# A two-layer block kernel on one core: gate tiles dealt 3, 2, 2, 1 between attention scores, and a first expert step whose rows TensorE picks

## The reference, cut to what matters

```python
def second_block(x, mem, ...):
    h = rmsnorm_2(x, norm_mix_g[l])
    u_glu, q, k, v, f_logit, gate_c, gate_a = jnp.split(h @ w_in[l], cuts, axis=-1)
    conv_out = conformer_conv(u_glu, ...)            # ends in silu(layernorm(u)) @ pw_w
    logf = jax.nn.log_sigmoid(f_logit + fox_bf[l])
    attn = fox_attention(q, k, v, logf)              # 8 heads of 64, causal, with a decay
    merged = sigmoid(gate_c) * conv_out + sigmoid(gate_a) * (attn @ attn_branch_w[l])
    x = x + merged @ w_out[l]
    x = x + cross_attention(...)
    x = x + hierarchical_moe(rmsnorm_2(x, norm_moe_g[l]), ...)

def fox_attention(...):
    s = q_i @ kh.T * scale + c_i[:, None] - c[None, :]     # c: running sum of logf
    p = softmax(where(kpos <= qpos, s, -inf))
    o = p @ vh

def hierarchical_moe(h, ...):      # 16 experts in 4 groups, two experts for each token
    combine = one_hot(expert_idx) * weights
    u = silu(h @ w_gate[e]) * (h @ w_up[e]) * combine      # w_gate, w_up: 1024 x 256
    y = sum over e of u @ w_down[e]                        # w_down: 256 x 1024
```

## Time and profile before

| | us |
|---|---|
| median of 3 runs | 1931.56 (1930.52 to 1934.93) |
| the profiled execution | 1928.75 |
| its span (first to last instruction) | 1927.0 |

### The profile page before, as it was taken

One profiled execution on the slowest core, in us unless ns is written; L12 is line 12 of the kernel. 1 busy time (PEld: TensorE's weight loads), 2 busy tenths in 40 slices (PEclk: granted clock), 3 DMA queues, 4 the chain that ended last, 5 costly groups with the idle time before them and its releaser, 6 DMA issues. The chain is left out here.

```text
span 1927.0 us, 18124 instructions
## 1 busy us (share of the span) xinstructions
PE 1730.1 (90%) x6987; PEld 788.3 (41%) x6987; DVE 554.9 (29%) x1088; ACT 385.4 (20%) x700; POOL 24.0 (1%) x34
## 2 busy tenths in 40 slices
PE   6998999999989999999999899978999999457882
PEld 4544545554436443444443334423444334212220
DVE  4605403551124011101111159553110113410113
ACT  5102113431022110010100310166300112300112
POOL 0100000000000000000000000000000000100001
PEclk9998999999999999999999999989999999778996
DMA  9611364111323999999999803111112131489965
GB/s 368 240 44 44 110 218 174 45 66 46 129 87 133 409 419 423 425 421 420 421 422 425 308 2 129 44 44 44 44 44 87 54 120 66 162 253 361 306 212 182
DMA packets 97193, 383.05 MB, mean 199 GB/s; under 512 B 11284, under 2 KB 11620, under 8 KB 86628
## 3 DMA queue, kind: packets, MB, share of 16 engines
q1 hardware_dynamic: 87268, 350.14, 47.3%
q10 hardware_dynamic: 5824, 17.30, 2.9%
q0 software_dynamic: 4032, 14.68, 2.0%
HBM read 467.03 MB, written 18.87 MB: 252 GB/s over the span
## 5 line engine op out<-in xcount | busy, mean ns | idle before, releaser
L1738 PE MATMUL bank<-H,weight_slots 128*128 128x512 f32 (+1 forms) x1024 | 424.4, 575 | 4.1 <-ACT H L677 2.9
L1738 PEld LDWEIGHTS bank<-H,weight_slots 128*128 128x128 f32 x1024 | 197.4, 194 | 226.0 <-issue 220.3
L1738 PE MATMUL bank<-R,weight_slots 128*128 128x512 f32 x576 | 250.9, 594 | 4.4 <-DVE R L1285 2.1
L1738 PEld LDWEIGHTS bank<-R,weight_slots 128*128 128x128 f32 x576 | 108.4, 190 | 143.2 <-issue 133.8
L2064 PE MATMUL bank<-weight_slots,SM 128*64 128x512 f32 x640 | 143.9, 595 | 9.4 <-DMA weight_slots<-in_w_up_e 9.4
L2390 PE MATMUL bank<-weight_slots,SM 128*32 128x512 f32 x768 | 98.3, 659 | 34.2 <-DMA weight_slots<-in_expert_w_up 33.4
L2092 PE MATMUL bank<-weight_slots,SM 128*64 128x512 f32 x384 | 113.7, 604 | 3.4 <-DMA weight_slots<-in_w_down_e 3.4
L1738 PE MATMUL bank<-R 128*128 128x128 f32 (+2 forms) x720 | 95.8, 286 | 3.5 <-ACT R L964 2.0
L1738 PEld LDWEIGHTS bank<-R 128*128 128x128 f32 x720 | 87.0, 195 | 6.9 <-issue 4.4
L2064 PEld LDWEIGHTS bank<-weight_slots,SM 128*64 128x64 f32 x640 | 45.4, 137 | 104.3 <-issue 84.2
L1738 PE MATMUL bank<-weight_slots,H 128*128 128x512 f32 x192 | 82.9, 592 | 0.0
(11 more groups left out here) (419 smaller groups left out, 1525.1 us busy)
## 6 DMA issues: line engine op xcount, KB each, us to landing
weight_slots<-in_expert_w_gate SPq DMA_DIRECT2D x102, 512.0 KB
weight_slots<-in_expert_w_up SPq DMA_DIRECT2D x102, 512.0 KB
R<-in_expert_w_down SPq DMA_DIRECT2D x51, 1024.0 KB
weight_slots<-in_w_up_e SPq DMA_DIRECT2D x24, 2048.0 KB, 17.3
weight_slots<-in_w_down_e SPq DMA_DIRECT2D x24, 2048.0 KB, 23.7
weight_slots<-in_w_in SPq DMA_DIRECT2D x18, 2048.0 KB, 10.2
weight_slots<-in_w_gate_e SPq DMA_DIRECT2D x16, 2048.0 KB, 17.0
weight_slots<-in_w_ada SPq DMA_DIRECT2D x12, 2048.0 KB, 10.6
```

The source lines that it names most:

```text
L1738: ins = nc.tensor.matmul(dst, lhsT, rhs, start=(i == 0), stop=(i == len(pairs) - 1))
```

## The change

Attention: the gate tiles are dealt otherwise among the pairs, on PE and on ACT alike, and both ends of the convolution move one pair later. Experts: the rows of step 0 are no longer read back from `x_rows`; PE picks and transposes them in one, as products of `h2_stage` with a table of zeros and ones that DVE makes from the slots (`pick_rows`). `load_rows(0)` goes. The list `rows_in` is rearranged so that nothing lands in `h2_stage`'s memory early.

```diff
@@ ScalarE
                 if hp + 1 < FOX_H // 2:
                     cb_copy(hp + 1)
+                    if hp == 0:
+                        gate_c(0)
                     probs(hp + 1)
+                    gate_c(2 * hp + 1)
+                    gate_c(2 * hp + 2)
                 else:
                     scale_probs(FOX_H * TT - 1)
-                gate_c(2 * hp)
-                gate_c(2 * hp + 1)
+                    gate_c(2 * hp + 1)
...
-                if hp == 1:
+                if hp == 2:
                     conv_silu()
...
-            for q in range(4):
+            for q in range(1, 4):
                 load_rows(q)
@@ VectorE
-                if hp == 1:
+                if hp == 2:
                     norm_conv()
...
+            step(nc.vector.tensor_tensor(pos_in, pos2.unsqueeze(3).broadcast_to([P, 2, TT, NSLOT]),
+                                         column_row.unsqueeze(1).unsqueeze(1).broadcast_to([P, 2, TT, NSLOT]), ALU.subtract))
+            in_block = iota[:, 0:BLK].unsqueeze(1).unsqueeze(1).broadcast_to([P, TT, NSLOT, BLK])
+            for a, rows in enumerate((first_rows, second_rows)):
+                nc.vector.tensor_tensor(rows.rearrange("p t (c r) -> p t c r", c=NSLOT), in_block, pos_in[:, a, :, :].unsqueeze(3).broadcast_to([P, TT, NSLOT, BLK]),
+                                        ALU.is_equal).then_inc(sem("first_hits"), 1)
+            dve.wait_ge(sem("first_hits"), 2)
+            nc.vector.tensor_tensor(first_rows, first_rows, second_rows, ALU.add).then_inc(sem("first_hits"), 1)
@@ TensorE
                     decays(hp + 1)
                     logits(hp + 1, (0, 1))
-                    if hp == 0:
-                        gate_c(1)
+                    gate_c(2 * hp + 1)
                     logits(hp + 1, (2, 3))
-                if hp:
-                    gate_c(2 * hp)
+                    gate_c(2 * hp + 2)
+                else:
                     gate_c(2 * hp + 1)
                 pe.wait_ge(sem("P_ready"), 8 * (hp + 1))
...
+            def pick_rows():
+                pe.wait_ge(*reached("h_rows", TT))
+                pe.wait_ge(sem("first_hits"), 3)
+                for i in range(2):
+                    for k in range(4):
+                        c = 128 * (4 * i + k)
+                        ins = product(PS[i][:, 128 * k:128 * (k + 1)], [(h2_stage[:, t, c:c + 128], first_rows[:, t, :]) for t in range(TT)])
+                    ins.then_inc(sem("q_turn_x"), 1)
...
-            turn_rows(0)
+            pick_rows()
@@ tables
-        rows_in = [a[:, D * i:D * (i + 1)] for a, n in ((R5, 2), (R6, 4), (h_flat[:, 4096:6144], 2), (x_flat, 4)) for i in range(n)]
+        rows_in = [a[:, D * i:D * (i + 1)] for a, n in ((R5, 2), (h_flat[:, 4096:6144], 2), (x_flat, 4), (R6, 4)) for i in range(n)]
```

More of the change, by code:

```diff
@@ L104 @@
 SHARED = {"product_done": bases(PRODUCT_STAGES), "copy_done": bases(COPY_STAGES), "vector_done": bases(VECTOR_STAGES)}
-CONST = {"ident": 0, "ones": 128, "s_le_j": 256, "s_ge_j": 384, "future": 512, "dft": 640, "iota": 896, "pick": 960, "fold": 962, "desc": 982, "column": 986, "first": 990, "thresh": 994, "both_norms": 1010, "final_norm": 1011, "eps2": 1012}
-NCONST = 1013
+CONST = {"ident": 0, "ones": 128, "s_le_j": 256, "s_ge_j": 384, "future": 512, "dft": 640, "iota": 896, "pick": 960, "fold": 962, "desc": 982, "column": 986, "first": 990, "thresh": 994, "both_norms": 1010, "final_norm": 1011, "eps2": 1012, "column_row": 1013}
+NCONST = 1017
 def constant_tables():
@@ L135, in constant_tables @@
     table[:, 1012] = EPS * EPS
+    table[:, 1013:1017] = BLK * NQUAD * other
     n, m = np.arange(T // 2)[:, None], np.arange(T)[None, :]
@@ L372, in build @@
         column, first, thresh = (const[:, CONST[n]:CONST[n] + k] for n, k in (("column", NG), ("first", NSLOT), ("thresh", T // BLK)))
+        column_row = const[:, CONST["column_row"]:CONST["column_row"] + NSLOT]
+        pos_in = R7[:, 2256:2256 + 2 * TT * NSLOT].rearrange("p (a t c) -> p a t c", a=2, c=NSLOT)
+        first_rows = R7[:, 3072:3072 + T].rearrange("p (t s) -> p t s", t=TT)
+        second_rows = R7[:, 3584:3584 + T].rearrange("p (t s) -> p t s", t=TT)
         desc = const[:, CONST["desc"]:CONST["desc"] + 4].unsqueeze(1).broadcast_to([P, TT, 4])
@@ L2365, in _ @@
             ins.then_inc(sem("rank_mm"), 1)
+            def pick_rows():
[6 more added lines that the diff above has]
+                    ins.then_inc(sem("q_turn_x"), 1)
             def turn_rows(q):
-                pe.wait_ge(sem(f"rows_in{q % 4}"), 16 * NSLOT * (q // 4 + 1))
+                pe.wait_ge(sem(f"rows_in{q % 4}"), 16 * NSLOT * (q // 4 + (1 if q % 4 else 0)))
                 for i in range(2):
```

## The result

| | us |
|---|---|
| before, median of 4 runs | 1933.24 (1930.52 to 1936.82) |
| after, median of 4 runs | 1909.18 (1905.75 to 1914.79) |
| ratio | 0.9877, 95% interval 0.9847 to 0.9907 |
| profiled executions, before and after | 1928.75 and 1908.44 (spans 1927.0 and 1906.7) |

The change takes 24 us off the median (18 to 30), where 26.6 had been forecast. Between the two profiled executions it is 20.3 us. In a later job, beside the experiments, the same kernel had 1912.96 (4 runs) against 1933.55 (9 runs): 0.9902, 0.9873 to 0.9932.

The account below looks back on a forecast made before the run. TensorE's waits in the attention and the step-to-step chain at the experts' start were taken as the bound; 19.2 us plus 7.4 make 26.6, from median 1931.56 to 1904.9 us, own range 1901 to 1910, wider range 1898 to 1915.

Parts of the forecast that it names:

- clock rival: Attention: the granted clock falls in the new stalls, two to four costing 2.2 to 3.8 us each; 1909 to 1920, chance 0.14.
- Pair 0: Attention, first pair: value part starts 1.6 us earlier behind gate tile 2, and runs warm, 2.2 us shorter.
- Pairs 1 and 2, up to the value part: Attention: 20.5 us from one value part to the next, gaining 1.6 and 7.5 us, with a 1.9 us stall.
- Pairs 1 and 2, the value part: Attention: the value part was taken at 8.53 us, with no loss of clock in the sum.
- Pair 3: Attention, last pair: one gate tile instead of two, 8.4 us against 14.7, gaining 6.3; sigmoid covered by 1.2 us.
- The prediction's last sentence: Signs of being wrong: clock falling at stalls, gate tile 7 waiting for ACT, or step 1's weights not equally earlier.
- Table switches: ScalarE in the attention: each table load costs 1.28 us, the next activation 0.01 us behind, without further drain.
- the rival that rested on it: ScalarE in the attention: each exposed table switch drains 1.38 us more, 8.5 us in all; 1913, chance 0.05.
- Experts, the start: Second experts: pick of 7 to 14 us, tables 2.4 us later, first gate_up 7.4 us earlier, 20.7 behind the slots.
- Experts, the end: Second experts: the start's whole 7.4 us reaches the end, bounds 1.9 and 8.8.
- From then on all is a chain: Experts after the first gate_up: gate_up, load, gate_up move along together, keeping the 7.4 us.
- the rival of the late weights: Experts: step 0's weights come with the last of the backlog, gaining 1.9 us instead of 7.4; 1910.4, chance 0.10.

Follow-up runs that it names:

- attn_only: The kernel before with only the attention part of the change; 1916.13 us against 1935.62, ratio 0.9898.
- conv_moved: The kernel before with only the convolution's two ends (norm on VectorE, silu on ScalarE) one pair later, gate tiles unchanged; 1930.07 us against 1935.62, ratio 0.9967.
- experts_only: The kernel before with only the experts part of the change; 1923.68 us, ratio 0.9937.

## Why the prediction was right

The forecast of 26.6 us stands against 24 (18 to 30) and, in the later job, 19 (13 to 25). The direction held, and the stalls and the early start came at the places that were named; the sum was too high in both halves. The trace gives the attention 15.3 us where 19.2 had been forecast (13.5 in attn_only), and the experts 6.2 us in the profiled pair, 2.4 in the mean of all traces, where 7.4 had been. Between the profiled executions that is 20.3 us, so that the median came as near as 24 is in part luck. The measured 1909.18 also lies in both the forecast's own range (1901 to 1910) and that of the clock rival (1909 to 1920), and the first of the prediction's signs of being wrong, a fall of the granted clock at the stalls, did come.

*Pair 0.* 1.6 and 2.2 us forecast. From gate tile 1 to the value part it is 18.92 us instead of 20.36, 1.4; the value part took 8.54 instead of 10.69, 2.15. Both held.

*Pairs 1 and 2, up to the value part.* 1.6 and 7.5 us forecast; from the end of one value part to the start of the next it is 20.58 us both times, against 22.07 and 28.05: 1.5 and 7.5. The stall was 1.92 as written. The split that the prediction gives for its 7.5 doesn't hold: both orders have two gate tiles there, none fewer. By the rows it is 3.5 us of stalls (4.13, 0.58 and 0.73 less 1.92) and 3.9 us that scores and gate tiles no longer lose at the low clock (16.10 us for two tiles before, 14.2 after). Up to 3.0 of it comes from conv_silu alone, as conv_moved showed.

*Pairs 1 and 2, the value part.* Here a term was missing from the sum. I took 8.53 us, and it is 10.23 and 10.26, since the clock fell: 1.7 us each. It was a rival (two to four stalls that cost 2.2 to 3.8 us each, chance 0.14) and came true at two of the stalls, at the smaller price of 1.7. The argument against it, that pair 0 had had a much longer stall, was no argument, because pair 0 had lost 2.2 us to it.

*Pair 3.* 6.3 us forecast, 14.73 to 8.56 measured: 6.2. Gate tile 7 waited for the copy of bank 5 (0.69), and the cover of ScalarE's sigmoid was 1.44 us where I had 1.2. The prediction's last sentence names this wait as a sign of being wrong, while its own working has it; it cost nothing beyond the sum.

*Table switches.* The rows after show the load of 1.28 us and the activation 0.02 us behind it (1291.61, 1292.91), as those before. The Trainium skill, "ScalarE: Activation LUTs", section "What ACT_TABLE_LOAD costs", adds 1.38 us of drain to each. At these switches the trace doesn't show it; the rival that rested on it (1913 us) is refuted here by the pairs' times, which fit without it, and ScalarE isn't idle ahead of the load either: its last scaling ends where the load starts.

*Experts, the start.* The first gate_up 20.7 us behind the slots was forecast, 20.8 came, and 20.7 to 21.9 in six more traces. The pick took 10.20 us between the bounds of 7 and 14. The tables came 2.15 us later behind the slots, SyncE's first load 2.3, against 2.4.

*Experts, the end.* "From then on all is a chain" is the step that was too strong. In the profiled pair 4.8 us of the lead arrived at the last gate_up (the 6.2 at the end hold 1.4 us that lie behind it), over all traces 2.4. The bounds (1.9 to 8.8) hold this, and the rival of the late weights (1.9 us, chance 0.10) came half true: not the first half of step 0's weights but the second was caught in the backlog. I had read one window of DMA share 0.18 and taken the engines to be idle from there on; their share was 0.88 again 10 us later and 0.93 to 1.03 after that. That the profiled pair came so near to the 7.4 was luck: the trace of after has one of the earliest ends of the seven, and that of before the latest of the three.

What stays open: why the medians of the parts add to more than the whole, and how much of the experts' gain is the earlier start. Executions of one kernel differ by 4 to 12 us, so four runs may be all there is to the first; it wasn't tested. This spread goes with TensorE's clock: of 29 executions of the kernel before in the three jobs of the experiments, the four under 1928 us had a mean granted clock of 0.957 to 0.960, the others (from 1930.44) 0.951 to 0.956.

## What to carry to other kernels

Idle time ahead of a stretch is not worth its length alone: count the clock with it, and try a stall of TensorE closed as well as shortened, since here only closing it paid. If an engine must switch tables to release a bank, let another engine with slack copy the bank out and do the function later in one go (9.0 us of the attention in the trace here). And before a lead is carried along a chain to the end, look at the DMA share of the whole way: here 6.5 us at the start were 2.4 at the end.

## What the runs showed of the hardware

- A stall of TensorE of 0.20 us, in a stretch that is busy otherwise but for two waits of 0.36 in each pair's value part, went with as much loss of clock as one of 1.92 us: 1.7 us once in each of pairs 1 and 2. Without it there was no fall in these pairs. Stalls of 0.73 us ahead of value parts before, and of 0.69 and 0.73 in pair 3 after, cost none.
- Where the fall is seen isn't where the idle time is: with 1.92 us it lay 2 us behind the stall, with 0.20 us some 11 us behind it.
- With 64 records of 128x128 TensorE took 10.20 us in after (clock 0.58 and 0.76 in the two windows of 10 us behind the slots), and 9.43 where it started 2.9 us later; 9.01 in the first experts.
- With the same code for the experts, the way from the token slots to the last gate_up differs by up to 4.7 us from trace to trace (203.8 to 208.5). In all but experts_only the order of the ends is nearly that of step 1's start (34.3 to 39.5).
